# Latent attention: the rotary quarters exchanged by VectorE instead of by a TensorE product

## The reference

```python
def apply_rope(x, cos, sin):
    half = x.shape[-1] // 2
    x1, x2 = x[..., :half], x[..., half:]
    return jnp.concatenate([x1 * cos - x2 * sin, x2 * cos + x1 * sin], axis=-1)

q = (rmsnorm(c_q, q_norm_g) @ w_uq).reshape(B, T, MLA_HEADS, MLA_NOPE + MLA_ROPE)
kv = (rmsnorm(c_kv, kv_norm_g) @ w_ukv).reshape(B, T, MLA_HEADS, MLA_NOPE + MLA_V)
q_nope, q_rope = q[..., :MLA_NOPE], q[..., MLA_NOPE:]
k_nope, v = kv[..., :MLA_NOPE], kv[..., MLA_NOPE:]
q_rope = apply_rope(q_rope, cos[:, :, None, :], sin[:, :, None, :])
k_rope = apply_rope(k_rope, cos, sin)
o = causal_mla_attention(q_nope, q_rope, k_nope, k_rope, v)   # 8 heads
```

## Time and profile before

| | |
|---|---|
| median of 3 runs | 2376.18 us (2374.58 to 2378.06) |
| the profiled execution | 2376.76 us, of which 2374.9 us are the span of the trace |
| TensorE busy | 2301.6 us, 97% |
| VectorE busy | 1334.2 us, 56% |
| ScalarE busy | 936.0 us, 39% |
| GpSimd busy | 371.0 us, 16%, nearly all in the first third |
| mean granted clock of TensorE | 0.995 of full speed |

### The profile page before, as it was taken

How to read it: one execution, slowest core, us unless ns; L and a number is a source line. 1 busy time by engine, 2 the same in 40 slices (tenths; PEclk the granted TensorE clock), 3 DMA queues, 4 the chain that set the end, 5 groups by cost and what they waited for, 6 DMA issues and landing times.

```text
span 2374.9 us, 32501 instructions
## 1 busy us (share of the span) xinstructions
PE 2301.6 (97%) x13527; PEld 1900.8 (80%) x13527; DVE 1334.2 (56%) x1657; ACT 936.0 (39%) x1275; POOL 371.0 (16%) x164
## 2 busy tenths in 40 slices
PE   6999999999999999999999999999999999999998
PEld 4677878888878886668888888888777788898887
DVE  4766755542376565547763466434367345864365
ACT  4546553442313354434332235344255324332232
POOL 0346456357780000000000000000000000000000
PEclk9999999999999999999999999999999999999999
DMA  7433232334442324311333232211211222223232
GB/s 298 141 113 137 107 116 90 124 142 177 185 187 87 110 76 155 124 54 71 107 104 109 90 112 106 89 53 71 89 54 56 87 89 76 103 102 111 89 107 89
DMA packets 40749, 260.40 MB, mean 110 GB/s; under 512 B 4432, under 2 KB 6832, under 8 KB 10416
## 3 DMA queue, kind: packets, MB, share of 16 engines
q1 hardware_dynamic: 40624, 258.59, 30.2%
HBM read 256.42 MB, written 2.15 MB: 109 GB/s over the span
## 4 chain that ended last, share of the span: by engine, by line
PE 72%; POOL 10%; issue 6%; DVE 5%; ACT 3%; DMA 1%; POOLq 0%; DVEq 0%; ACTq 0%
PE D L301 8%; PE D L302 8%; PE D L303 8%; POOL adar L375 6%; POOL adar L373 5%; PE D L1626 3%; PE D L1625 3%; PE D L1624 3%; PE D L1663 3%; PE D L1661 3%; PE D L1662 3%; PE D L2817 2%; PE D L1399 1%; PE D L2819 1%; PE D L2818 1%
## 5 line engine op out<-in xcount | busy, mean ns | idle before, releaser
L366 DVE TENSOR_TENSOR lo<-raw,hi 128x2048 fp32r<-128x2048 f32 (+3 forms) x136 | 300.9, 2213 | 202.4 <-ACT hi L362 202.3
L362 ACT ACTIVATE hi<-raw 128x2048 fp32r<-128x2048 f32 (+3 forms) x136 | 239.7, 1762 | 365.4 <-PE D L303 267.9
L301 PE MATMUL D<-hH,lo 128*128 128x512 f32 x640 | 258.8, 404 | 5.5 <-DVE lo L366 5.5
L302 PE MATMUL D<-hL,hi 128*128 128x512 f32 x640 | 252.4, 394 | 0.0
L303 PE MATMUL D<-hH,hi 128*128 128x512 f32 x640 | 252.4, 394 | 0.0
L375 POOL TENSOR_TENSOR adar<-adar 128x1024 f32<-128x1024 f32 (+2 forms) x120 | 215.0, 1791 | 9.4
L373 POOL TENSOR_TENSOR adar<-adar,small 128x2048 f32<-128x2048 f32 x40 | 156.6, 3915 | 322.6 <-DVE zi L1285 187.3
L301 PE MATMUL D<-aH,lo 128*128 128x512 f32 x390 | 155.1, 398 | 0.0
L302 PE MATMUL D<-aL,hi 128*128 128x512 f32 x390 | 154.6, 396 | 0.0
L303 PE MATMUL D<-aH,hi 128*128 128x512 f32 x390 | 154.4, 396 | 0.0
L301 PEld LDWEIGHTS D<-hH,lo 128*128 128x128 f32 x640 | 120.6, 188 | 36.1 <-DVE lo L366 7.0
(11 more groups left out here) (544 smaller groups left out, 5506.0 us busy)
## 6 DMA issues: line engine op xcount, KB each, us to landing
raw<-in_slabs SPq DMA_DIRECT2D x185, 1024.0 KB, 4.8
adar<-in_ada SPq DMA_DIRECT2D x42, 1024.0 KB, 4.8
fw<-in_ada SPq DMA_DIRECT2D x6, 1024.0 KB, 22.8
x<-in_xin SPq DMA_DIRECT2D x2, 1024.0 KB, 9.0
dt<-bcast SPq DMA_DIRECT2D x8, 256.0 KB, 3.3
dtb<-bcast SPq DMA_DIRECT2D x8, 256.0 KB, 3.5
qd<-bcast SPq DMA_DIRECT2D x8, 256.0 KB, 3.8
out<-x SPq DMA_DIRECT2D x8, 256.0 KB, 2.2
```

Of the source, the lines that this page charges most:

```text
L301: T_.matmul(o, lo[s.slot][:, w], H[:, k, :], start=(k == 0), stop=False)
L302: T_.matmul(o, hi[s.slot][:, w], L[:, k, :], start=False, stop=False)
L362: S_.activation(hi[s.slot][:, 0:n], raw[s.slot][:, 0:n], ACT.Copy).then_inc(hi_ready, 1)
L366: V_.tensor_tensor(lo[s.slot][:, 0:n], raw[s.slot][:, 0:n], hi[s.slot][:, 0:n], ALU.subtract).then_inc(lo_ready, 1)
```

## The change

TensorE's two kinds of swap product go (`key_swap_pe` and the product in `mla_steps`; the step stays, empty). VectorE makes the exchange in the multiplication by the sine: four instructions on 32 partitions and 512 columns each, that read one quarter of the source and of `msin` and write the other quarter of the destination. Since the sign of `msin` is then that of the source's row, the sum becomes a difference. All four are linked. TensorE's first half of k waits for ScalarE's copy of bank 0, no longer for the turned queries. A helper `rope_parts` is defined and nothing calls it.

```diff
-        def key_swap_pe(pe):
-            pe.wait_ge(tab_in, 32)
-            pe.wait_ge(bank_free[Slab(G_MIN + 2).slot], Slab(G_MIN + 2).prior(1))
-            T_.matmul(D[3][:, 0, :], swp[:, 0:P], craw[:, 5, :], start=True, stop=True).then_inc(ms["ksw"], 1)
...
                     yield from latent(q, 0, 2, 1, range(3), ms["half_done"])
-                    out_of(pe, p, 0)
-                    T_.matmul(D[0][:, 0, :], swp[:, 0:P], qr0[:], start=True, stop=True).then_inc(ms["sw"], 1)
                     yield
                     w("half_free", 3 * p + 1)
                     yield from latent(q, 1, 2, 1, range(3), slab_done)
                     pe.wait_ge(lo_ready, k.plus(1))
                     if p == 0:
                         w("cL", 5)
-                    w("qr", p + 1)
+                    out_of(pe, p, 0)
                     yield from latent(k, 0, 2, 0, (3, 4), ms["half_done"])
...
             fill(3)
-            key_swap_pe(pe)
             fill(12)
...
+            def swapped(dst, src):
+                for a in range(0, P, 64):
+                    for to, of in ((a, a + 32), (a + 32, a)):
+                        L(V_.tensor_tensor(dst[to:to + 32], src[of:of + 32], msin[of:of + 32, :], ALU.mult))
+
             def queries_turned(p):
-                w("sw", p + 1)
                 out_of(dve, p, 0)
                 r = qrs[p % 2]
                 V_.tensor_tensor(r, qr0[:], mcos[:], ALU.mult)
-                L(V_.tensor_tensor(craw[:, 5, :], D[0][:, 0, :], msin[:], ALU.mult))
-                V_.tensor_tensor(r, r, craw[:, 5, :], ALU.add).then_inc(ms["qr"], 1)
+                swapped(craw[:, 5, :], qr0[:])
+                V_.tensor_tensor(r, r, craw[:, 5, :], ALU.subtract).then_inc(ms["qr"], 1)
...
-            w("ksw", 1)
+            last = Slab(G_MIN + 2)
+            dve.wait_ge(bank_free[last.slot], last.prior(1))
             L(V_.tensor_tensor(krp[:], craw[:, 5, :], mcos[:], ALU.mult))
-            L(V_.tensor_tensor(mrs[:], D[3][:, 0, :], msin[:], ALU.mult))
-            V_.tensor_tensor(krp[:], krp[:], mrs[:], ALU.add).then_inc(ms["kr"], 1)
+            swapped(mrs[:], craw[:, 5, :])
+            V_.tensor_tensor(krp[:], krp[:], mrs[:], ALU.subtract).then_inc(ms["kr"], 1)
             queries_turned(0)
             next_lo(0, 3)
             keys_in(0, 0)
```

More of the change, by code:

```diff
@@ L2021, in ffn_dve @@
             final_dve(dve, g + N_GUB, gate, 2 * f + 1)
-        ms = {n: sem("m_" + n) for n in ("ang", "trig", "sq", "ss", "rs", "cn", "cH", "cL", "ksw", "kr", "sw", "qr", "sc",
+        ms = {n: sem("m_" + n) for n in ("ang", "trig", "sq", "ss", "rs", "cn", "cH", "cL", "kr", "qr", "sc",
                                          "mx", "ex", "pn", "tr", "pt", "pv", "half_done", "half_free", "c4")}
@@ L2471, in build @@
         b_col = lambda o, i=None, step=0: vec[:, bass.ds(at(V["b_in"] + o, i, step), 1)]
-        pairs = lambda ap: ap.unsqueeze(1).to_broadcast([P, 2, T])
+        pairs = lambda ap: ap.unsqueeze(1).to_broadcast([ap.shape[0], 2, T])
         def rope_dve(chain, dst, raw_, cos_, sin_, swapped=None, tmp=None):
@@ L2479, in rope_dve, with rope_parts @@
             return V_.tensor_tensor(dst[:], dst[:], tmp[:], ALU.add)
+        def rope_parts(chain, n, dst, raw_, cos_, sin_, tmp):
+            V_.tensor_tensor(dst[:], raw_[:], pairs(cos_), ALU.mult)
+            for a in range(0, P, 2 * n):
+                for to, of in ((a, a + n), (a + n, a)):
+                    chain.link(V_.tensor_tensor(tmp[to:to + n], raw_[of:of + n], pairs(sin_[of:of + n, :])[:], ALU.mult))
+            return V_.tensor_tensor(dst[:], dst[:], tmp[:], ALU.subtract)
         def ret_pe(pe):
```

## The result

The changed kernel takes 2383.37 us (median of 20 runs, 2377.22 to 2384.22) against 2376.36 us (20 runs, 2373.96 to 2378.62). The ratio is 1.0025, 95% interval 1.0018 to 1.0031: slower by 5.9 us by the ratio, 7.0 by the medians. The forecast was 4.0 us more, 2380.2; the range ended at 2383.2, so the median lies just above it; the ratio on the 2376.18 that the forecast started from gives 2382.1, inside it. The profiled execution took 2382.55 us.

A forecast was written before the change was run, and what follows sets the result against it. The kernel was taken to be bound by TensorE's queue of products. The terms 1.1 + 1.5 + 0.95 + 0.4 = 3.95, say 4.0 us, on the median 2376.18 gave 2380.2 us; the range with rivals was 2376.6 to 2383.2.

The forecast's parts named there:

- The price of a narrow instruction: VectorE's 32x512 multiplications: 0.68 us each, 0.72 us from start to start when linked, judged from the 32x384 copy's 539 ns.
- The rival of cheap narrow instructions: Partitions count, so narrow instructions are spaced as little as 0.33 us: -4.3 us, 2371.9; chance 0.07.
- The first pair: VectorE's longer turning of key and queries delays TensorE's values: +1.1 us, plus +1.5 us for the clock.
- The clock's 1.5 us: First pair: after a longer idle time ahead of v, TensorE's clock falls during v, +1.5 us (bounds nothing to 2.9).
- the rival of the full clock: First pair: the clock stays full in v, so only +2.5 us in all, 2378.7; chance 0.15.
- The second pair: Later maxima delay scaling and ScalarE's copy of q, so k's second half starts late: +0.95 us, swap product's 0.86 counted.
- The fall of the clock in the second pair: Rival: TensorE idles 1.7 in 2 us around the transposes and its clock falls, 1.5 us more, 2381.7; chance 0.15.
- the 1.3 us that cost nothing: Idle time at 1020 to 1022 before the change, after which the clock stayed at 1.00; yardstick for the clock rivals.
- The third and fourth pair: Turning begins later after the swap, hiding more delay: k's second half +0.2 us late in each, 0.4 in all.
- The rest of the kernel: Behind these places all is TensorE's queue, so nothing later can win the loss back.

The follow-up runs named there:

- e1: Kernel before with only the key turned by narrow instructions, queries keeping their swap products; 2379.80 us, ratio 1.0011.
- e2: Changed kernel with the key's swap product back, so only the queries are turned by narrow instructions; 2379.54 us, ratio 1.0010.
- e3: Changed kernel with the four narrow multiplications made one of 128x512 without the exchange, for timing only; 2370.85 us, ratio 0.9978.
- e8: Changed kernel with the first three of the four narrow instructions issued without a wait between them; 2381.43 us, ratio 1.0021.
- e6: Changed kernel with swap products back for key and first pair, the first pair's in a bank of its own; 2377.51 us, ratio 0.9998.
- e7: Changed kernel with key and first pair by swap products, the latter in its own bank, and later pairs' turning moved to units 5 and 6; 2374.05 us, ratio 0.9989.

## Why the prediction was right, and where it was short

- **The price of a narrow instruction** was right: 683 ns, 0.72 from start to start. The copy of 32x384 was the row to go by. The rival of cheap narrow instructions is refuted by that row of after.
- **The first pair** was right term by term in the profiled execution: values 1.18 us later against the copy of `qr0` (forecast 1.1), then 1.43 us for the clock (forecast 1.5), first score 2.61 us later (2.6). e1 and e2 share the delay between the key (2.14 us in front of k) and the queries, and e3 shows that with a short VectorE it is a gain. The clock's 1.5 us have luck in them: in e8 the same wait of 3.21 us had no fall behind it, so there the rival of the full clock, with a chance of 0.15, came true. The wait was to be 4.5 us; it was 3.21, since the fall behind the wait ahead of q, which the prediction does not have, made k end later.
- **The second pair**: the wait for the scaling and for the copy of q came where I put them. From the first score to the second half of k it took 938.72 - 921.27 = 17.45 us against 935.60 - 919.23 = 16.37: +1.08 us where I gave +0.95.
- **The fall of the clock in the second pair** I held for a rival with a chance of 0.15. It is in the traces of after, e2 and e6, and not in that of e8. Against the same place in e8 it costs 1.7 us in after, 3.2 in e2 and 1.6 in e6. This is the step that was mis-sized: I compared 1.7 us of idle time with "the 1.3 us that cost nothing", and took the mild side. That 1.3 was also misread. It is what the stretch from 1020 to 1022 shows of a wait that went on behind it, and the rows of before have a second long wait:

```profile
1022.21 0.33 PE L2249 MATMUL D<-cst,pr 128*128 128x128 f32 x1 [1.53 <-DVE pr L2426]
...
1044.89 0.77 PE L2249 MATMUL D<-cst,pr 128*128 128x128 f32 x4 [1.94 <-DVE pr L2426]
```

Behind the first the clock stayed full, behind the second it fell (0.57 from 1045 to 1049). With the fall in the second pair the sum is 4.0 + 1.7 = 5.7, close to the 5.9 measured by the ratio.
- **The third and fourth pair** were right: from the start of k's second half in one to that in the next it takes 34.19 us (938.72 to 972.91, with the fall of the clock in it) and 32.65 us (972.91 to 1005.56), against 32.42 in the kernel before (968.02 to 1000.44). The last two differ by 0.23 (forecast 0.2).
- **The rest of the kernel** gave nothing back, as forecast. The fall of the clock near the end of the stage, from 1045 to 1049 before, stands at 1028 to 1031 in the changed kernel, behind the wait of 1.54 us that is the 1.53 of before.

The twenty executions of the changed kernel spread over 7 us, and the three shortest (2377.22, 2379.20, 2379.23) have mean granted clocks of 0.994 to 0.995, all others 0.990 to 0.993. That fits falls that are there in one execution and not in the next, as after and e8 show for two of them. Only the profiled executions show where they are. Counted over them, with other edits around the same waits: behind the 1.45 us of the second pair a fall came in three traces of four (after, e2 and e6, not e8), behind the 1.53 us of the fourth pair in four of eleven (e7 has no such wait), behind the 1.94 us near the end of the stage in five of twelve. So in these traces the length of a wait does not settle whether the clock falls behind it, and how often each fall occurs stays open.

## What to carry to other kernels

A narrow instruction of 512 columns cost VectorE here what a full one costs, so work that moves from one product to four narrow instructions is paid by whoever is queued behind them: read that queue, not the engine's busy share of 56%. When a change takes a dependence away (here k no longer needs the turned queries), move the work to where its result is next needed; left in its old place it cost 6 us, and moved, with the first pair's product in a free bank, it won 7, of which the bank alone wins 3. Before moving work to another engine, see whether a free buffer ends the wait. A wait of one and a half microseconds on TensorE should be priced twice, once as it stands and once with the clock's fall.

## What the runs showed of the hardware

- A two-input multiplication of 32x512 fp32, read from one group of 32 partitions and written to another, takes 678 to 689 ns (twenty in the trace of after), as much as one of 128x512 (685), whichever of the four groups it reads.
- Four of them on changing groups take 2.83 us with a wait after each and 2.83 us without (e8).
- A fall of TensorE's clock to 1.2 GHz followed waits of 3.21 us and of 1.45 plus 0.22 us in one execution and did not follow the same waits (3.21, and 1.44 plus 0.22) in another. It cost 1.4 and 1.7 us. Its length differed: the one of e2 stood at 0.50 from 938 to 944 and cost 3.2 us, that of e7 lasted from 1009 to 1020 though TensorE was busy for nearly all of it.
